# Second mixer of a two-block transformer kernel: values stationary, three branches summed in one bank, weights scaled by GpSimd

## What is computed

```python
q, kc, vc, ks, vs, kw, vw, gates, z = jnp.split(h @ w_in, cuts, axis=-1)
kcmp, vcmp = compress(kc, ...), compress(vc, ...)      # 15 blocks of keys and values
o_cmp = softmax(q @ kcmp.T / 8) @ vcmp
o_slc = softmax(q @ ks.T / 8) @ vs                     # here: every key that is not in the future
o_win = softmax(q @ kw.T / 8) @ vw                     # here: the same mask
g = sigmoid(gates)
o = g[0] * o_cmp + g[1] * o_slc + g[2] * o_win         # per head
return (o * silu(z)) @ w_out
```

## Time and profile before

| | us |
|---|---|
| median of 3 runs | 2271.07 (2269.82 to 2271.65) |
| the profiled execution's own time | 2271.82 |
| its span | 2270.5 |
| TensorE busy (PE) | 2206.2 |
| VectorE busy (DVE) | 1463.9 |
| ScalarE busy (ACT) | 1078.8 |
| GpSimd busy (POOL) | 175.9 |

### The profile page before, as it was taken

How to read it: one execution, slowest core, us unless ns; L and a number is a source line. 1 busy time by engine, 2 the same in 40 slices (tenths; PEclk the granted TensorE clock), 3 DMA queues, 4 the chain that set the end, 5 groups by cost and what they waited for, 6 DMA issues and landing times.

```text
span 2270.5 us, 27331 instructions
## 1 busy us (share of the span) xinstructions
PE 2206.2 (97%) x10659; PEld 1803.4 (79%) x10659; DVE 1463.9 (64%) x1919; ACT 1078.8 (48%) x1599; POOL 175.9 (8%) x318
## 2 busy tenths in 40 slices
PE   6889999999998999999999999999999999999998
PEld 5777788888887888888888888877778877877777
DVE  6767878888875566565554456566665536666664
ACT  3234356544446534444443544555555524565544
POOL 0004311122210000000000000000000000000000
PEclk8889999999998999999999999999999989999999
DMA  9997866788885677777555555544445633333333
GB/s 344 331 305 271 302 206 230 252 307 304 305 288 164 228 238 238 229 237 226 185 185 192 179 193 178 186 149 149 149 154 185 215 123 126 107 112 113 110 130 130
DMA packets 242165, 468.53 MB, mean 206 GB/s; under 512 B 14363, under 2 KB 52469, under 8 KB 241397
## 3 DMA queue, kind: packets, MB, share of 16 engines
q1 hardware_dynamic: 213552, 387.74, 51.9%
q0 software_dynamic: 20480, 67.13, 8.7%
q10 hardware_dynamic: 8004, 11.93, 1.5%
HBM read 464.65 MB, written 2.10 MB: 206 GB/s over the span
## 4 chain that ended last, share of the span: by engine, by line
PE 88%; DVE 5%; issue 2%; ACT 2%; DMA 2%; POOL 1%; SPq 0%; ACTq 0%; DVEq 0%
PE banks L625 26%; PE banks L627 25%; PE banks L626 25%; PE banks L637 2%; PE banks L913 2%; PE banks L925 1%; DVE ada_acc_vec L1735 1%; DMA ada_w<-in_w_ada 1%; ACT w_high L1163 1%; DVE w_low L1676 1%; PE banks L940 1%; PE banks L939 1%; PE banks L1028 1%; PE banks L938 1%; DVE ada_acc L1696 1%
## 5 line engine op out<-in xcount | busy, mean ns | idle before, releaser
L1676 DVE TENSOR_TENSOR w_low<-raw,w_high 128x1024 fp32r<-128x1024 f32 x674 | 821.9, 1224 | 625.7 <-ACT w_high L1163 625.2
L1163 ACT CAST w_high<-raw 128x1024 fp32r<-128x1024 f32 x674 | 701.4, 1046 | 791.4 <-PE banks L627 791.1
L625 PE MATMUL banks<-w_high,act_a_high 128*128 128x512 f32 (+1 forms) x1696 | 691.2, 408 | 21.7 <-DVE act_a_low L1768 14.2
L626 PE MATMUL banks<-w_low,act_a_high 128*128 128x512 f32 (+1 forms) x1696 | 668.3, 394 | 0.0
L627 PE MATMUL banks<-w_high,act_a_low 128*128 128x512 f32 (+1 forms) x1696 | 668.1, 394 | 0.0
L625 PEld LDWEIGHTS banks<-w_high,act_a_high 128*128 128x128 f32 x1696 | 326.6, 193 | 103.9 <-issue 21.6
L627 PEld LDWEIGHTS banks<-w_high,act_a_low 128*128 128x128 f32 x1696 | 326.3, 192 | 69.5
L626 PEld LDWEIGHTS banks<-w_low,act_a_high 128*128 128x128 f32 x1696 | 326.6, 193 | 63.1 <-issue 2.4
L625 PE MATMUL banks<-w_high,act_b_high 128*128 128x512 f32 x640 | 250.7, 392 | 0.0
L627 PE MATMUL banks<-w_high,act_b_low 128*128 128x512 f32 x640 | 249.1, 389 | 0.0
L626 PE MATMUL banks<-w_low,act_b_high 128*128 128x512 f32 x640 | 249.0, 389 | 0.0
(11 more groups left out here) (338 smaller groups left out, 2013.5 us busy)
## 6 DMA issues: line engine op xcount, KB each, us to landing
raw<-in_w_ff SPq DMA_DIRECT2D x128, 1024.0 KB, 5.2
raw<-in_w_in SPq DMA_DIRECT2D x64, 1024.0 KB, 7.0
ada_w<-in_w_ada POOLq DMA_DIRECT2D x256, 256.0 KB, 4.8
raw<-in_b_w_in SPq DMA_DIRECT2D x44, 1024.0 KB, 5.1
raw<-in_a_w_in SPq DMA_DIRECT2D x36, 1024.0 KB, 5.1
ada_first<-in_w_ada SPq DMA_DIRECT2D x64, 512.0 KB, 9.0
raw<-in_w_o SPq DMA_DIRECT2D x16, 1024.0 KB, 7.1
raw<-in_a_w_out SPq DMA_DIRECT2D x16, 1024.0 KB, 5.2
```

What stands on the lines that cost most here:

```text
L625: T.matmul(out, xh, wh, start=(c.first and k == 0), stop=False)
L626: T.matmul(out, xh, wl, start=False, stop=False)
L1163: A.copy(WH[:, h % SPL, :, :], split_ap(h)).then_inc(*done("high", h))
L1676: V.tensor_tensor(WL[:, h % SPL, :, :], split_ap(h), WH[:, h % SPL, :, :].bitcast(F32), ALU.subtract).then_inc(*done("low", h))
```

## The change

- Each pair of the second mixer now stands for two heads in the selected (even i) or the window branch (odd i), so that the two pairs of the same heads follow one another (`BRANCHES`).
- VectorE makes a factor, gate over row sum, for each pair (`gate_factor`, three steps behind the scores); the gates are multiplied with half the inverse rms once. GpSimd multiplies the weights in `sc` by it, four instructions a pair: 128 and 256 columns for each of two heads.
- `pair_values` has the values stationary and 256 and 128 columns of `pt` moving, 4 products for a pair. For each even pair a product of the compressed branch with 256 columns opens the sum in bank 3; so all three branches of two heads are summed there, transposed.
- z is transposed into bank 2 in two lots of four at steps 18 and 21 and copied by ScalarE to `zT` (`z_turn`, `z_store`). VectorE multiplies bank 3 with it (`out_gate`, 128x256), ScalarE and VectorE split the result (`out_high`, `out_low`). `cmp_values`, `oo_begin`, `add_outputs`, `oo_gate` and the turning of `oo` are gone.
- The exponentials are one step behind the scores instead of two, and in ScalarE's order of one step they stand ahead of the copy of a turned pair, in both mixers.

```diff
@@ tables @@
-OO_STEP = 40
+EXP = {"a": 2, "b": 1}
+BRANCHES = {"a": 1, "b": 2}
+Z_STEPS = {"a": (18, 23), "b": (18, 21)}
@@ pool_program @@
+        for g in range(GROUPS):
+            for i in range(PAIRS["b"]):
+                G.wait_ge(*of("scores_exp", ("b", g, i)))
+                G.wait_ge(*of("rd_step", ("b", g, i, 1)))
+                for e in range(2):
+                    for tt in range(NT):
+                        c0, n = (0, P) if tt == 0 else (P, SEQ)
+                        w = sc[:, 2 * (i % 2) + e, c0:c0 + n]
+                        G.tensor_scalar(w, w, rd[:, 2 * (i % 4) + e, tt:tt + 1], None,
+                                        ALU.mult).then_inc(*done("weights_scaled", ("b", g, i)))
@@ tensor_program @@
-            T.wait_ge(*of("weights_scaled" if name == "a" else "scores_exp", (name, g, i)))
+            T.wait_ge(*of("weights_scaled", (name, g, i)))
...
+            j, first, last = i // BRANCHES[name], i % BRANCHES[name] == 0, (i + 1) % BRANCHES[name] == 0
+            if first:
                 T.wait_ge(*emptied[3])
+            if first and name == "b":
+                T.wait_ge(*of("cpt_made", g))
+                T.matmul(bank(3)[:, 0:SEQ], vbd[0:HB, g, j * P:(j + 1) * P], cpt[0:HB, :, :].rearrange("p a n -> p (a n)"),
+                         start=True, stop=False)
             for e in range(2):
-                T.matmul(o0, pt[:, s, 0:P], v0, start=True, stop=True)
-                T.matmul(o1, pt[:, s, P:2 * P], v0, start=True, stop=False)
-                mm = T.matmul(o1, pt[:, s, 2 * P:3 * P], v1, start=False, stop=True)
+                T.matmul(bank(3)[e * HD:(e + 1) * HD, 0:SEQ], v0, pt[:, 2 * (i % 2) + 1 - e, 0:SEQ],
+                         start=(name == "a"), stop=False)
             for e in range(2):
                 mm = T.matmul(bank(3)[e * HD:(e + 1) * HD, P:SEQ], v1, pt[:, 2 * (i % 2) + 1 - e, 2 * P:3 * P],
+                              start=False, stop=last)
...
+        def z_turn(name, g, half):
+            T.wait_ge(*of("pair_free", (name + "_z", g)))
+            if emptied[2] is not None:
+                T.wait_ge(*emptied[2])
+            transposes(2, zs, 2 * half * P).then_inc(*done("z_turned", (name, g, half)))
+            emptied[2] = of("z_stored", (name, g, half))
@@ scalar_program @@
             for i in range(PAIRS[name]):
+                if rel == score_step(name, i) + EXP[name]:
+                    pair_exp(name, g, i)
+            for i in range(PAIRS[name]):
                 if rel == turn_step(name, i):
                     pair_store(name, g, i)
-            for i in range(PAIRS[name]):
-                if rel == score_step(name, i) + 2:
-                    pair_exp(name, g, i)
+            if rel in Z_STEPS[name]:
+                z_store(name, g, Z_STEPS[name].index(rel))
@@ vector_program @@
+        def gate_factor(g, i):
+            br, j, o = i % 2, 2 * (i // 2), 2 * (i % 4)
+            hs, g0 = slice(o, o + 2), 32 * (br + 1) + GH * g + j
+            V.wait_ge(*of("scores_exp", ("b", g, i)))
+            V.reciprocal(rd[:, hs, :], sm[:, br, j:j + 2, :]).then_inc(*done("rd_step", ("b", g, i, 0)))
+            V.wait_ge(*of("rd_step", ("b", g, i, 0)))
+            V.tensor_tensor(rd[:, hs, :], rd[:, hs, :], gts[:, :, g0:g0 + 2].rearrange("p a h -> p h a"),
+                            ALU.mult).then_inc(*done("rd_step", ("b", g, i, 1)))
```

More of the change, by code:

```diff
@@ L1120, in cmp_turn @@
             emptied[3] = of("cpt_made", g)
-        def cmp_values(g):
-            for b in (2, 3):
-                T.wait_ge(*emptied[b])
-            T.wait_ge(*of("cpt_made", g))
-            for tt in range(NT):
-                mm = T.matmul(bank(2 + tt), cpt[0:HB, tt, :], vbd[0:HB, g, :], start=True, stop=True)
-            mm.then_inc(*done("cmp_valued", g))
-            for b in (2, 3):
-                emptied[b] = of("oo_begun", (g, b - 2))
         for s, (c, k) in enumerate(stage_steps(C, "b")):
@@ new lines, in out_low, with out_hooks @@
+        def out_low(name, g, j):
+            H, L = (CHI, CLO) if name == "a" else (DHI, DLO)
+            k = GH // 2 * g + j
+            V.wait_ge(*of("out_high", (name, g, j)))
+            V.tensor_tensor(L[:, k, :], gated[:, j % 2, :], H[:, k, :].bitcast(F32),
+                            ALU.subtract).then_inc(*done("out_low", (name, g, j)))
+        def out_hooks(name, g, rel):
+            for j in range(GH // 2):
+                if rel == gate_step(name, j):
+                    out_gate(name, g, j)
+                if rel == gate_step(name, j) + 1:
+                    out_low(name, g, j)
@@ L2184, in vector_program @@
                 rel = s - GROUP * g
-                for i in range(PAIRS["a"]):
-                    if rel == gate_step(i):
-                        out_gate(g, i)
-                    if rel == gate_step(i) + 1:
-                        out_low(g, i)
+                out_hooks("a", g, rel)
                 for i in range(PAIRS["a"]):
@@ L2276, in vector_program @@
         V.wait_ge(*of("pair_free", ("b_gates",)))
-        V.tensor_scalar(gts[:, :, :], gts[:, :, :], 0.5, 0.5, ALU.mult, ALU.add).then_inc(*done("gates_made"))
+        V.tensor_scalar(gts[:, :, :], gts[:, :, :], 0.5, 0.5, ALU.mult, ALU.add).then_inc(*done("gates_made", 0))
+        V.wait_ge(*of("gates_made", 0))
+        for tt in range(NT):
+            V.tensor_scalar(gts[:, tt, :], gts[:, tt, :], rh[:, tt:tt + 1], None, ALU.mult).then_inc(*done("gates_made", 1))
+        V.wait_ge(*of("gates_made", 1))
         for k in range(KT):
@@ L2366, in vector_program @@
                     cmp_weights(g)
-                if rel == 12:
-                    oo_begin(g)
+                for i in range(PAIRS["b"]):
+                    if rel == score_step("b", i) + 3:
+                        gate_factor(g, i)
                 for i in range(PAIRS["b"]):
```

147 lines of the change are left out of this document (37 added, 110 removed).

## The result

| | before | after |
|---|---|---|
| median of 4 runs each | 2271.36 us | 2317.78 us (2316.82 to 2319.54) |
| span of the profiled execution | 2270.5 | 2316.0 |

The changed kernel is slower: ratio 1.0206, 95% interval 1.0189 to 1.0224. The direction is the one forecast; the loss is 46 us instead of 23, just past the end of the range at 2316.

The account below looks back on a forecast made before the run. The prediction took TensorE, busy for 97% of the span, as the bound, so its issued work plus waits set the time. Its terms summed to +22.7 us: 2294 against the median of 2271.1, own range 2281 to 2308, stated range 2268 to 2316.

Parts of the forecast that it names:

- Part 1: Second mixer's turn and values: 1.61 us instead of 1.91, 0.30 less for each of 32 pairs, -9.6 us.
- Part 2: Compressed branch: two products of 512 columns per group become four of 256, 0.53 us each, +8.5 us.
- Part 3: Gate's transposes: z's added lots cost +3.6 us; removed output transposes save 2.6 us at the late output chunk.
- Part 5: Turns of pairs 2 and 3 wait for ScalarE's copy of z, 2.4 and 1.4 us per group, +15.3 us.
- Part 7: TensorE's waits ahead of value products, for the adding of outputs, disappear: -1.4 us.
- Part 4: Opening of a group: work disappears, but a chain to pair 0's copy holds up pair 2's scores; +1.1 us in all.
- Part 6: Last pair of a group: its factor stands behind the query rotation, a wait of 2.6 us in three groups, +7.8 us.
- Part 8: GpSimd's four multiplies per pair take 1.6 us and cost nothing in steady pairs, with 2.2 us of room.
- forecast's own sign of being wrong: Wrong if z's copy is there at the turn, pair 2 starts 3 us sooner, or GpSimd's four take over 2.2.
- third rival: VectorE's split blocks GpSimd's scaling, 1.2 us per pair, +14 us: 2308, or 2373 at the higher price; 15%.
- second rival: No change: opening gains 1.5 to 2 us per group, last pair waits 1, z +11: about 2274 us; 12%.
- first rival: Faster: lighter VectorE removes the lateness, opening gains 13 us, last pair waits for nothing, z +10.4: 2266 us; 13%.

Follow-up runs that it names:

- e2: The changed kernel with ScalarE's copy of turned z ahead of the exponentials of the same step, second mixer only: 2304.18 us.
- e1: The changed kernel without GpSimd's scaling; weights go unscaled into the products and a pair's turn waits for its factor on VectorE: 2285.85 us.
- e4: The changed kernel with TensorE's idle time ahead of the turns of pairs 0, 2, 3, 5 and 7 filled with useless products: 2307.08 us.
- e11: The order of e9 with the scaling left out altogether, so weights go unscaled into the products: 2254.74 us.
- e5: The changed kernel without scaling, second mixer's copies of z and of a turned pair placed ahead of the exponentials of the same step: 2270.54 us.
- e3: The changed kernel with the weights scaled by VectorE right behind the factor, two instructions a pair, none on GpSimd: 2316.82 us.
- e7: The changed kernel with the weights scaled by ScalarE, ahead of the next pair's exponentials, and nothing on GpSimd: 2297.44 us.
- e13: e9 with VectorE gating a group's third lot of outputs ahead of the rotation of the next queries: 2258.18 us.
- e8: e7 with the copy of z first, the last pair's factor a step sooner, and pair 0's copy ahead of exponentials in its step: 2282.87 us.
- e9: e8 with pair 1's exponentials a step later, the last pair's scaling ahead of the next queries, and pair 0's factor a step sooner: 2269.70 us.
- e10: The order of e9 with GpSimd scaling as in the changed kernel: 2285.24 us.

## Why the forecast was wrong in size

Part by part, from the mixer's first scores on:

- **Part 1, value products:** right. 1.58 us per pair against 1.61 forecast.
- **Part 2, compressed branch:** right. 0.52 against 0.53. **Part 3:** right at the late output chunk, where the gap fell from 2.6 to 0.2; the added transposes were not priced by themselves.
- **Part 5, z behind the exponentials:** right. Waits of 2.4 and 1.3, 14.9 us in all against 15.3, and 13.6 us came back when the copy went first (e2). **Part 7:** right; no wait for the adding of outputs is left.
- **Part 4, the opening:** the chain was right and its size near, in a kernel without GpSimd's share: e1 has pair 2's scores 0.7 us later than before (0.3 forecast). Left out was that pair 0's turn itself would wait for the scaling, 3.0 us, which takes the place of the chain's wait (0.2 left of 2.6).
- **Part 6, the last pair:** the place was right, the size 4.8 instead of 2.6. e1 has 0.8 us of it, which is the late factor; the rest is GpSimd, whose four take 3.8 us there.
- **Part 8, GpSimd: this is the step that failed.** "Four per pair: 1.6 to 5.5 us. I take 1.6" rested on a selection of 0.40 us, another operation. The scaling takes 3.0, and 4.2 with a split in it, so that the forecast's own sign of being wrong, four over 2.2 us, came true. "From 2.2 on every excess is waited for" failed as well: the room was 2.7 at pair 5 and 2.9 or more at pairs 1, 3, 4 and 6, so that 3.0 fitted there. The third rival had a part of the mechanism: a split meets the scaling at pair 5 (1.2 us, a wait of 1.6) and at pair 7 (0.8). But most of the cost fell on pairs 0 and 7, where the chain is short, by the length of the multiplies themselves: 0.60 and 0.96 us where the forecast had 0.40.
- **Missing: the clock.** No term stood for it. Idle time was forecast at some 40 us and came out at 49.9; but the stretches at half clock behind the long waits cost 15 us more (e4).
- **The second rival is added up wrongly:** with its own terms, -6, +3 and +11, the sum is +6.5 and the time 2278, not 2274. By the forecast's own 0.2% that is slower and no longer the same; the forecast's sum and range do not rest on it.

The sum with these: 22.7 forecast, + (34.8 - 7.8 in part 6 - 10.3, the wait of e1 at pair 2's scores that it replaces) = 16.7 for GpSimd, + 15 for the clock = 54, against 49.6 measured. Some 5 us in the other direction stay unplaced. The first rival was near what the form is worth: it put everything except z at -14.5, and e11, with the order mended and the scaling left out, is 13.9 us shorter than before from the mixer's first scores to the end. No run takes that number apart into its terms, so how close the two are may be luck. It decides where the forecast said it would, at the opening and at z's waits, but only once pair 1's exponentials stand behind the copy of pair 0.

Not settled: why the clock falls after some waits and not after others of the same length. The kernel before has one such stretch as well, 3.4 us at 0.50 from 2051 on, in which products start 0.43 us apart; TensorE's longest wait near it is 0.5 us, ten microseconds ahead. So a long wait is not the only way there. In e5 the same wait of 2.6 us ahead of pair 2's scores stands in four groups, and half clock follows in three, as the windows behind the four waits show (the clock is the third number from the end):

```profile
1913.40:1917.00 3.60, 3.55 (x13) 2.55 (x14) 2.60 (x6) 0.90 (x1) 0.00 (x0) 0.56 0.55 149
1990.80:1994.00 3.20, 3.10 (x13) 2.37 (x14) 2.88 (x8) 0.95 (x1) 0.00 (x0) 0.64 0.48 109
2068.40:2072.00 3.60, 3.55 (x20) 2.79 (x21) 3.28 (x8) 1.24 (x3) 0.00 (x0) 1.00 0.54 142
2145.00:2149.00 4.00, 4.00 (x15) 2.82 (x16) 3.19 (x8) 1.16 (x3) 0.00 (x0) 0.57 0.54 170
```

## What to carry to other kernels

Price a new operation on GpSimd by a row of that very operation, and if there is none, keep the upper bound in the sum where the chain is shortest: the first and the last item of a loop, not its steady middle. A step that another engine waits for is paid by its length and by its place in its queue; moving it to a faster engine gains nothing if it then stands ahead of the next item's first step (e3), and a slower place costs nothing if the engine would have waited there anyway (e7, e13). And a wait of TensorE near 3 us is priced with the half clock that may follow it: here 15 us for eight stretches, 1.9 us each; even waits of 2 us had it at times (e8, e9, e10).

## What the runs showed of the hardware

- GpSimd's multiply by a column of factors, fp32, takes 0.60 us for 128 columns and 0.92 to 0.96 for 256; ScalarE's copy with a scale is listed at 0.39 and 0.49 us, and a VectorE multiply of 512 columns at 0.68.
- A split of 1.22 us on VectorE lengthened GpSimd's four by 1.2 us (3.0 to 4.2), the whole of it; one that met them in part, by 0.8 (3.8, pair 7).
- TensorE idle for 3.0 us: granted clock 0.50 for 5.6 us, in which weight products start 0.43 us apart instead of 0.23. Of twenty waits of up to 2.1 us, 19 left it at 1.00 and one of 1.98 did not (e10); of four waits of 1.8 to 1.9 us, three had half clock behind them (e8). In the kernel before it was 0.50 for 3.4 us with no wait over 0.5 us near.
